# Attention core of a hybrid trunk: the products of weights and values move ahead of the transposes within a slot

## The reference

```python
h = h + 0.5 * swiglu_ffn(rmsnorm(h, ffn1_norm[i]), ffn1_w_in[i], ffn1_w_out[i])
u = rmsnorm(h, mix_norm[i])
y = stick_breaking_attention(u, sb_w_qkv[j], sb_w_o[j], valid)
h = h + y
h = h + 0.5 * swiglu_ffn(rmsnorm(h, ffn2_norm[i]), ffn2_w_in[i], ffn2_w_out[i])
h = rmsnorm(h, final_norm)

# within the attention, for each block of 128 queries and the keys before them:
z = einsum('bhqd,bhkd->bhqk', q, k)               # q scaled by 128 ** -0.5
# A[t, s] = sigmoid(z_ts) * prod_{s < j < t} (1 - sigmoid(z_tj)),  s < t
w = where(before & valid, exp(log_w), 0.0)        # log_w = log A
out = einsum('bhqk,bhkd->bhqd', w, v)             # then out @ w_o
```

## Time and profile before

| | |
|---|---|
| median of three runs | 2162.15 us |
| profiled execution | 2163.53 us, its span 2161.7 us |
| PE busy over the span | 1971.6 us (91%) |
| DVE, ACT, POOL busy | 1084.0, 688.9, 1004.1 us |
| mean granted TensorE clock | 0.968 |
| attention core | from 1077 to 1314 us of the span |
| seven head periods (start of S0 to the next) | 26.98, 29.36, 28.40, 28.51, 29.95, 28.48, 28.42 us |

### The profile page before, as it was taken

The page is one execution under the profiler, slowest core; times in us unless marked ns, Lnnn a source line. Parts: engine busy times, 40 slices in busy tenths (PEclk is TensorE's granted clock), DMA queues, the critical chain, the costliest instruction groups (busy, mean ns, idle before and its releaser), DMA issues.

```text
span 2161.7 us, 35352 instructions
## 1 busy us (share of the span) xinstructions
PE 1971.6 (91%) x12808; PEld 1793.3 (83%) x12808; DVE 1084.0 (50%) x1584; ACT 688.9 (32%) x1226; POOL 1004.1 (46%) x671
## 2 busy tenths in 40 slices
PE   4699999999999967999888878959999999999997
PEld 4699999999999957999877777738777777778886
DVE  5455544444555564343277772155444444444445
ACT  5322222222111233222277773132223222221112
POOL 4554454455443525454466664154445445544340
PEclk8799999999999988999999999979999999999999
DMA  3122222223323201323322112002222222333221
GB/s 118 30 69 81 85 69 83 83 70 117 118 93 102 69 10 42 116 93 110 120 60 59 45 54 69 20 0 63 82 87 63 85 85 68 102 122 116 78 87 78
DMA packets 164783, 167.64 MB, mean 78 GB/s; under 512 B 7920, under 2 KB 130800, under 8 KB 164736
## 3 DMA queue, kind: packets, MB, share of 16 engines
q1 hardware_dynamic: 164736, 166.99, 24.3%
HBM read 126.74 MB, written 40.22 MB: 77 GB/s over the span
## 4 chain that ended last, share of the span: by engine, by line
PE 46%; issue 27%; POOL 19%; ACT 3%; DVE 3%; DMA 1%; POOLq 0%; DVEq 0%; ACTq 0%; SPq 0%
PE psum L1174 14%; PE psum L1175 14%; PE psum L1176 14%; POOL arena L514 13%; POOL arena L522 4%; PE psum L1201 2%; PE psum L1324 1%; ACT psum L818 1%; ACT scratch L816 1%; DVE scratch L1092 1%; DVE arena L1057 1%; PE psum L1354 1%; DVE psum L897 0%; ACT scratch L876 0%; DMA scratch<-w_out_dram 0%
## 5 line engine op out<-in xcount | busy, mean ns | idle before, releaser
L1174 PE MATMUL psum<-arena 128*128 128x260 f32 (+4 forms) x4008 | 1283.1, 320 | 123.7 <-POOL arena L522 93.3
L1176 PE MATMUL psum<-arena 128*128 128x260 f32 (+4 forms) x4008 | 1265.8, 316 | 0.0
L1175 PE MATMUL psum<-arena 128*128 128x260 f32 (+4 forms) x4008 | 1264.3, 315 | 0.0
L1174 PEld LDWEIGHTS psum<-arena 128*128 128x128 f32 x4008 | 762.8, 190 | 190.0 <-issue 99.8
L1176 PEld LDWEIGHTS psum<-arena 128*128 128x128 f32 x4008 | 762.1, 190 | 47.0
L1175 PEld LDWEIGHTS psum<-arena 128*128 128x128 f32 x4008 | 762.0, 190 | 45.7 <-issue 3.1
L514 POOL TENSOR_TENSOR arena<-scratch,arena 128x512 fp32r<-128x512 f32 x371 | 512.4, 1404 | 564.7 <-ACT arena L655 564.7
L655 ACT ACTIVATE arena<-scratch 128x512 fp32r<-128x512 f32 x392 | 224.1, 622 | 516.1 <-DMA scratch<-w_in_dram 262.5
L957 DVE SCALAR_TENSOR_TENSOR h<-psum,h 128x260 f32<-128x260 f32 (+1 forms) x528 | 272.1, 516 | 223.3 <-PE psum L1176 223.2
L969 DVE TENSOR_TENSOR scratch<-scratch,psum 128x520 f32<-128x520 f32 (+1 forms) x280 | 193.0, 689 | 370.8 <-PE psum L1176 356.6
L972 DVE TENSOR_TENSOR scratch<-scratch 128x512 f32<-128x512 f32 x212 | 252.1, 1189 | 235.1 <-POOL arena L514 210.6
(11 more groups left out here) (72 smaller groups left out, 934.4 us busy)
## 6 DMA issues: line engine op xcount, KB each, us to landing
scratch<-w_in_dram SPq DMA_DIRECT2D x88, 512.0 KB, 4.9
scratch<-w_out_dram SPq DMA_DIRECT2D x22, 1024.0 KB, 4.9
qkv<-scratch SPq DMA_DIRECT2D x48, 260.0 KB, 2.1
scratch<-w_qkv_dram SPq DMA_DIRECT2D x24, 512.0 KB, 4.6
scratch<-qkv SPq DMA_DIRECT2D x24, 512.0 KB, 3.5
hidden<-scratch SPq DMA_DIRECT2D x44, 260.0 KB, 2.1
scratch<-hidden SPq DMA_DIRECT2D x11, 1040.0 KB, 5.0
hidden<-scratch SPq DMA_DIRECT2D x44, 256.0 KB, 2.1
```

Source lines behind the costliest of these rows:

```text
L1174: nc.tensor.matmul(dst, wh, xh, start=start, stop=False, skip_group_check=True)
L1175: nc.tensor.matmul(dst, wh, xl, start=False, stop=False, skip_group_check=True)
L1176: return nc.tensor.matmul(dst, wl, xh, start=False, stop=stop, skip_group_check=True)
```

## The change

In `head` (L1365) the call of `mix_values` moves from the end of a slot to the place straight behind `score` and `tail`, ahead of `transpose_weights` and `transpose_v`. In `tail` the two calls change places as well; but the tail's transposes stand in slots 0 to 2 and its products in slots 3 and 4 (M9 to M11 belong to an even block and issue nothing), so that no instruction of the tail moves.

```diff
             def tail(s, hd):
 
+                if s + S - W_LAG < S:
+                    mix_values(s + S - W_LAG, hd)
                 if s + S - T_LAG < S:
                     transpose_weights(s + S - T_LAG, hd)
-                if s + S - W_LAG < S:
-                    mix_values(s + S - W_LAG, hd)
 
             def head(hd, j, first=False):
                 for s in range(S):
                     score(s, hd, j, first)
                     if not first:
                         tail(s, hd - 1)
+                    if s >= W_LAG:
+                        mix_values(s - W_LAG, hd, first)
                     if s >= T_LAG:
                         transpose_weights(s - T_LAG, hd, first)
                     if s in VT_SLOTS:
                         transpose_v(VT_SLOTS.index(s), hd, first)
-                    if s >= W_LAG:
-                        mix_values(s - W_LAG, hd, first)
```

## The result

The changed kernel takes 2177.39 us (median of four runs, 2176.16 to 2177.48) against 2162.66 us for the kernel before beside it: ratio 1.0069, interval 1.0051 to 1.0086, 14.7 us slower. I had forecast 7.2 us. The direction was right; the size was half of what came, and outside my range by 0.4 us.

What follows compares the result with a forecast made beforehand. It took each head to be bound by a loop of waits, no engine full. Slots 6, 9, 12 and 13 gave 0.25 + 0.45 + 0 + 0.2 = 0.9 us a head, 7.2 for eight: 2169.4 us, range 2164 to 2177.

Steps and rivals of the forecast that it cites:

- The path through ACT: Slots 6, 9, 13: ACT's high part, formerly hidden under products, now follows transposes behind them, ahead of the next sigmoid; slot 9 0.45 us.
- rival 4: Slot 6: products fill PE's stall before the values' low part is ready; at best 2158 us; chance 5%.
- the idle times before H: Sign on ACT: idle time before the high part about 1.4 us in slot 6, 1.2 to 1.3 in 9, 0.8 in 13.
- rival 1: Slot 9: the scan's later start on DVE is not covered; 0.8 us a head, 6.5 together, 2176 us; chance 9%.
- slot 6: Three weight transposes now caught behind the wait for the values delay the next scores: 0.25 us a head, bounds 0.15 and 0.4.
- slot 9: Transposes end last, so ACT's high part is no longer hidden under products: 0.45 us a head, bounds 0.35 and 0.5.
- slot 12: Products wait for the same low part as the transposes; ACT's idle time covers the delay: nothing, bounds 0 and 0.1.
- slot 13: As in slot 9 but with three tiles, delaying the next sigmoid: 0.2 us a head, bounds 0.1 and 0.35.
- rival 2: Slot 6: TensorE's clock falls in more heads, 7.5 us, 2177 (9%), or in fewer, 4 us less, 2165 (9%).
- signs of being wrong: Undisturbed head 28.5 us or less, PE's slot 6 idle time shrinking, or heads' clocks rather than waits carrying the difference.

Runs made afterwards that it cites:

- the runs with a steady clock: Kernel before with 14 added matmuls filling slot 6's stall and the changed order in one slot alone: slot 9 2164.2 us, slot 6 2162.9, slot 13 2157.4.
- slot 6 alone: Kernel before with the changed order in slot 6 only, its other slots as before: 2171.5 us against 2162.3, ratio 1.0044.
- the filled kernels: 14 matmuls of no use added in slot 6's stall: to the changed kernel 2166.0 us, to the kernel before 2160.0, each against 2162.3.

## Why the prediction was right in its waits and wrong in its time

The path through ACT held. PE doesn't do M1 in the stall (rival 4), since both waits name the same count; M1 starts at the stall's end. H moves from under the products onto the path; the idle times before H are 1.48, 1.20 and 0.72 us, where I had given 1.4, 1.2 to 1.3 and 0.8. The scan of slot 9 was covered (rival 1 fell), and the terms add from slot to slot: clean heads are 29.4 us.

The single terms, by the runs with a steady clock: slot 6 0.42 us where I took 0.25, slot 9 0.39 for 0.45, slot 12 0 to 0.05 for nothing, slot 13 0.09 for 0.2. The sum is 0.93 for 0.9. Slot 6 was mis-sized, to just over my upper bound of 0.4. From the end of L1047 to the end of S7 it was 2.25 us (1176.92 - 1174.67) and is 2.70 (1241.35 - 1238.65), 0.45 more. T3 holds the queue for 0.33 us (1240.28 - 1239.95), since more transposes follow it; the 0.25 that I took from T10 leave out what the first product behind transposes costs more, 0.20 instead of 0.12 us (1240.83 - 1240.63). That product is now the first of S7, 0.08 us more; M1 starts 0.08 us later behind L1047 and takes 1.17 us for 1.14; and V1, no longer first behind the idle time, takes 0.35 us for 0.42. I had named the extra 0.08 us after the idle time and after transposes as a bound and not counted them.

The step that failed is the weighing of rival 2, and with it the sum, which holds the waits alone and puts TensorE's clock at nothing. I priced a fall right, at 1.5 us, and its worst case of five more at 7.5 us, 2177. Behind the first head four more came, 6 us at that price. But I gave the rival 9%, on the ground that the stretch without a product gets shorter, from 2.75 to 2.33 us. The runs showed that this measure doesn't decide: slot 6 alone took the falls from two to six, and filling the stall took them to none. The length of the idle stretch doesn't decide either: it grew from 1.82 to 2.24 us, but with three transposes or products in it, which left 1.9 us in the fourth head, there were six falls too. One of my signs of being wrong came in part: of the 14.7 us the heads' clocks carry, by the filled kernels and within their wide intervals, more than the waits: 8.7 against 6.0. I also asked only how many heads fall, not how far apart. In the changed kernel the falls recur about every 30.7 us, and a head with a fall lasts 30.95; that one fall so puts the next head's stall in the way of the next is my reading, with the two lengthened versions of the changed kernel for it. The trace of before had a hint of the distance: its low stretches in the first and second heads begin at 1087.2 and 1118.0 us, 30.7 us apart.

What stays open: which feature of slot 6 makes it fall. Three transposes or three products in the stall don't prevent it, fourteen products do. With the four matmuls of S7 ahead of it there were none either, but there M1 stands ahead of V1 too, no products of S7 follow, and a head is shorter. The order M1, V1 alone gave four falls. T3 and V1 between M1 and S7, with the stall as it was, were not tested by themselves. The counts are from one profiled execution each, so a difference of one or two falls means little.

## What to carry to other kernels

Moving ready work ahead in a queue helps only if it isn't waiting for the same thing as what it overtakes; list both waits before counting the stall as free. What is overtaken has a consumer too: a piece that another engine had handled in the shadow of the long work comes into the open. And on a path that repeats, a stall that sometimes costs TensorE its clock is a risk to be priced for every repetition, not for the share that one trace shows. The cure that paid here was to draw independent work of the next step into it.

## What the runs showed of the hardware

- TensorE's clock fell to the lower level in slot 6 or 7 of six of the seven heads behind the first, around the end of an idle stretch of 2.24 us (2.5 in the last). With three transposes or products in the stall the idle stretches were 1.6 to 2.2 us and it fell in six as well; in the kernel before they were 1.5 to 2.2 us and it fell in two. With the stall of the changed kernel filled, 0.3 to 0.8 us of idle time left, it fell in none. A fall made a head 1.3 to 1.6 us longer (30.69 to 31.04 against 29.44 us).
- How many heads fall hangs on the length of the head too: in the changed kernel the falls began 30.7 us apart, and with four matmuls added to each head twice that. So making a loop longer can make it hardly slower: seven heads took 210.7 us in the changed kernel, 211.1 with four matmuls more in each (3.3 us of work) and 212.9 with eight (6.7 us).
- In slot 6, in the heads between the first and the last, a product that waits for L1047 starts 0.13 us behind its end, a transpose in its place 0.05 us.
- The Trainium skill, in "TensorE: Matmul & The Clock Gate", Part 4 (PE-mode transpose), gives about 275 ns for a 128x128 transpose in a kernel's context. The profile of the kernel before agrees in length (L1324, mean 276 ns over 352 of them). What one holds of the queue is less: three take 0.33 us before other transposes, and 0.25 before a product, which then takes 0.20 us to the next instead of 0.12.
